# First modulation rows: eight resident units, five summed by VectorE, three multiplied by TensorE, rows read from the accumulators

## The reference, cut to what matters

```python
mod = jax.nn.silu(c) @ w_ada + b_ada            # c: 1 x 1024, w_ada: 1024 x 6144
sh1, sc1, g1, sh2, sc2, g2 = jnp.split(mod, 6)
h = rms_norm(x, norm1_g) * (1 + sc1) + sh1
proj = h @ w_in
```

## Time and profile before

| | |
|---|---|
| Median of three runs | 2128.17 us (2126.04 to 2130.38) |
| The profiled execution | 2135.76 us, span 2132.9 us |
| TensorE busy | 1873.9 us (88%), 10004 records |
| VectorE busy | 1362.5 us (64%) |
| ScalarE busy | 911.1 us (43%) |
| DMA over the span | 403.91 MB, 189 GB/s |

### The profile page before, as it was taken

One profiled execution on the slowest core, in us unless ns is written; L12 is line 12 of the kernel. 1 busy time (PEld: TensorE's weight loads), 2 busy tenths in 40 slices (PEclk: granted clock), 3 DMA queues, 4 the chain that ended last, 5 costly groups with the idle time before them and its releaser, 6 DMA issues.

```text
span 2132.9 us, 25755 instructions
## 1 busy us (share of the span) xinstructions
PE 1873.9 (88%) x10004; PEld 1610.2 (75%) x10004; DVE 1362.5 (64%) x1848; ACT 911.1 (43%) x951; POOL 87.0 (4%) x101
## 2 busy tenths in 40 slices
PE   1897895688979989999999999979987779999997
PEld 0676774467869867999999999878966568878875
DVE  5458767655889855555555555556854368887885
ACT  1354423231123334444444444445533346666664
POOL 0000100000000033111000000000000000000000
PEclk9898956698989999999999999989987879999999
DMA  6543342341325477666655555544335148898892
GB/s 233 197 177 125 131 151 108 127 158 63 141 103 177 163 244 235 205 214 203 215 179 194 179 195 180 194 162 161 118 120 196 51 162 330 321 347 330 325 349 114
DMA packets 60590, 403.91 MB, mean 189 GB/s; under 512 B 7921, under 2 KB 8337, under 8 KB 14049
## 3 DMA queue, kind: packets, MB, share of 16 engines
q1 hardware_dynamic: 50976, 370.17, 47.4%
q0 software_dynamic: 5808, 20.29, 3.3%
q10 hardware_dynamic: 3730, 12.42, 1.7%
HBM read 390.79 MB, written 12.06 MB: 189 GB/s over the span
## 4 chain that ended last, share of the span: by engine, by line
PE 79%; DVE 13%; ACT 4%; issue 3%; DMA 2%; DVEq 0%; ACTq 0%; SPq 0%
PE ps L1944 20%; PE ps L1945 20%; PE ps L1946 20%; PE ps L2022 6%; PE ps L2257 3%; DVE wlo L1032 2%; ACT whi L582 2%; DMA raw<-in_stream_dram 2%; PE ps L2106 1%; PE ps L2430 1%; PE ps L2085 1%; PE ps L2495 1%; PE ps L2316 1%; PE ps L1968 1%; DVE H L1058 1%
## 5 line engine op out<-in xcount | busy, mean ns | idle before, releaser
L1032 DVE TENSOR_TENSOR wlo<-raw,whi 128x2048 fp32r<-128x2048 f32 x186 | 425.7, 2291 | 432.8 <-ACT whi L582 432.8
L582 ACT ACTIVATE whi<-raw 128x2048 fp32r<-128x2048 f32 x186 | 356.2, 1916 | 461.5 <-PE ps L1946 418.2
L1944 PE MATMUL ps<-thi,whi 128*128 128x256 f32 x1088 | 311.1, 286 | 5.1 <-DVE tlo L1044 4.2
L1945 PE MATMUL ps<-tlo,whi 128*128 128x256 f32 x1088 | 310.3, 285 | 0.0
L1946 PE MATMUL ps<-thi,wlo 128*128 128x256 f32 x1088 | 310.1, 285 | 0.0
L1944 PE MATMUL ps<-whi,thi 128*128 128x512 f32 (+1 forms) x584 | 236.4, 405 | 32.8 <-DVE wlo L1032 25.7
L1944 PE MATMUL ps<-whi,phi 128*128 128x512 f32 x608 | 243.1, 400 | 21.4 <-DVE plo L1508 15.0
L1945 PE MATMUL ps<-wlo,phi 128*128 128x512 f32 x608 | 241.1, 396 | 0.0
L1946 PE MATMUL ps<-whi,plo 128*128 128x512 f32 x608 | 240.0, 395 | 0.0
L1945 PE MATMUL ps<-wlo,thi 128*128 128x512 f32 (+1 forms) x584 | 231.1, 396 | 0.0
L1946 PE MATMUL ps<-whi,tlo 128*128 128x512 f32 (+1 forms) x584 | 230.9, 395 | 0.0
(11 more groups left out here) (374 smaller groups left out, 2685.8 us busy)
## 6 DMA issues: line engine op xcount, KB each, us to landing
raw<-in_stream_dram SPq DMA_DIRECT2D x272, 1024.0 KB, 4.8
BIG<-in_stream_dram SPq DMA_DIRECT2D x80, 1024.0 KB, 7.1
BIG<-g_spill POOLq DMA_DIRECT2D x64, 128.0 KB, 4.6
g_spill<-H ACTq DMA_DIRECT2D x4, 1024.0 KB, 4.8
g_spill<-MOD ACTq DMA_DIRECT2D x4, 1024.0 KB, 4.9
MID<-in_gains_dram POOLq DMA_DIRECT2D x7, 512.0 KB, 4.6
s_spill<-MOD ACTq DMA_DIRECT2D x10, 256.0 KB, 4.8
MOD<-in_b_ada_dram POOLq DMA_DIRECT2D x1, 2048.0 KB, 13.6
```

The source lines that it names most:

```text
L582: nc.scalar.activation(whi[:, u % 2, :], raw[:, u % 2, :], ACT.Copy).then_inc(unit_hi, 1)
L1032: nc.vector.tensor_tensor(wlo[:, u % 2, :], raw[:, u % 2, :], whi[:, u % 2, :].bitcast(f32), ALU.subtract).then_inc(unit_split, 1)
L1944: nc.tensor.matmul(out, ahi, bhi, start=start, stop=False)
L1945: nc.tensor.matmul(out, ahi, blo, start=False, stop=False)
```

## The change

The eight units of group 0 get eight buffers: seven in BIG (empty at this time) and one in MID. SyncE issues them at once, in six transfers (units 0, 1-2, 3-4, 5, 6, 7), each with its semaphore, and behind them, with no wait, the first two units of w_in. The raw buffers and the counts of unit_split now begin with w_in (`landed`, and "- DC" in the waits). VectorE sums units 0 to 4 only. TensorE multiplies units 5, 6 and 7 directly as float32, with silu_cols as the stationary side: a 128x128 block for each unit in which every column is silu(c)'s slice (a new copy by VectorE). The sum of the five is multiplied by ones, and b_ada by a one-row matrix of ones; all go into the same four accumulators, in the order b_ada, unit 5, sum, unit 6, unit 7. The copies into MOD and the memset of the accumulator go: VectorE reads shift and scale from the accumulators, with the 1 added to the scale in the same instruction. Its order becomes: five sums, norm, modulation, tr_low of groups 0 and 1, lo(U_IN), tr_low of groups 2 and 3, lo(U_IN + 1). Several semaphores for small steps are merged into two (small_logs, small_exps), with the same waits. The diff, cut to its core:

```diff
+def landed(at):
+    return 16 * ((at - DC) // 2 + 1)
...
+        ada_raw = [big[:, c * UW:(c + 1) * UW] for c in range(DC - 1)] + [mid[:, 0:UW]]
+        ADA_LOADS = ((0, 1), (1, 3), (3, 5), (5, 6), (6, 7), (7, 8))
+        ADA_SUMMED = 5
+        silu_cols = mid[:, UW:UW + DC * P].rearrange("p (c n) -> p c n", c=DC)
+        b_ada_row = MOD[0:1, 0:UW]
+        ada_starts = {first: k for k, (first, _) in enumerate(ADA_LOADS)}
+        first_shift, first_scale = (ps[:, k:k + 2, :].rearrange("p a n -> p (a n)") for k in (0, 2))
+        ada_acc = [mid[:, 3072:3072 + UW], H[:, :, :].rearrange("p t n -> p (t n)"), big[:, 0:UW]]
...
+            for k, (first, last) in enumerate(ADA_LOADS):
+                if last - first == 1:
+                    sp.dma_start(ada_raw[first], stream[first, :, :]).then_inc(ada_loaded[k], 16)
+                else:
+                    sp.dma_start(big[:, first * UW:last * UW].rearrange("p (a n) -> p a n", n=UW),
+                                 stream[first:last, :, :].rearrange("a p n -> p a n")).then_inc(ada_loaded[k], 16)
             for k in range(2):
-                sp.dma_start(raw[:, k, :], stream[k, :, :]).then_inc(raw_loaded[k], 16)
...
+                sp.dma_start(raw[:, k, :], stream[DC + k, :, :]).then_inc(raw_loaded[k], 16)
...
-                        sp.wait_ge(unit_split, 2 * i + (k - 1 - whole))
+                        sp.wait_ge(unit_split, 2 * i + (k - 1 - whole - DC))
...
-            act.wait_ge(ada_zeroed, 1)
-            act.dma_start(ada_acc[0][0:1, :], io["b_ada"][0:UW].rearrange("(a n) -> a n", a=1)).then_inc(b_ada_loaded, 16)
+            act.dma_start(b_ada_row, io["b_ada"][0:UW].rearrange("(a n) -> a n", a=1)).then_inc(b_ada_loaded, 16)
...
-            nc.vector.memset(ada_acc[0], 0.0).then_inc(ada_zeroed, 1)
             nc.vector.memset(ones, 1.0).then_inc(ones_ready, 1)
             dve.wait_ge(siluc_ready, 1)
-            dve.wait_ge(b_ada_loaded, 16)
+            nc.vector.tensor_copy(silu_cols, siluc.unsqueeze(2).broadcast_to([P, DC, P])).then_inc(ones_ready, 1)
...
-                    if g == 0:
-                        last = nc.vector.tensor_scalar(out, got, plus, None, ALU.add)
-                    else:
-                        last = nc.vector.scalar_tensor_tensor(out, got, plus, out, ALU.add, ALU.add)
-                    last.then_inc(ada_free, 1)
-            def first_rows():
-                for u in range(3, DC):
-                    ada_sum(u)
-                ada_rows(0)
-                dve.wait_ge(ada_free, 4)
-            for u in range(3):
-                ada_sum(u)
-            norm(0, X, rows_ready, sc1, sh1, first_rows)
+                    nc.vector.scalar_tensor_tensor(out, got, plus, out, ALU.add, ALU.add).then_inc(ada_free, 1)
+            def first_sum(c):
+                if c in ada_starts:
+                    dve.wait_ge(ada_loaded[ada_starts[c]], 16)
+                if c == 0:
+                    mark(nc.vector.tensor_scalar(ada_acc[0], ada_raw[c], siluc[:, 0:1], None, ALU.mult))
+                    return
+                settle()
+                last = nc.vector.scalar_tensor_tensor(ada_acc[0], ada_raw[c], siluc[:, c:c + 1], ada_acc[0],
+                                                      ALU.mult, ALU.add)
+                if c < ADA_SUMMED - 1:
+                    mark(last)
+                else:
+                    last.then_inc(ada_summed, 1)
+            for c in range(ADA_SUMMED):
+                first_sum(c)
+            norm(0, X, None)
+            dve.wait_ge(ada_full, 1)
+            for t in range(TT):
+                settle()
+                mark(nc.vector.scalar_tensor_tensor(H[:, t, :], first_scale, 1.0, H[:, t, :], ALU.add, ALU.mult))
+                settle()
+                nc.vector.tensor_tensor(H[:, t, :], H[:, t, :], first_shift, ALU.add).then_inc(rows_ready, 1)
+            tr_low(T_H1, 0, (0, 1))
             lo(U_IN)
+            tr_low(T_H1, 0, (2, 3))
             lo(U_IN + 1)
-            tr_low(T_H1)
...
-            ada_sums(0, DC)
+            pe.wait_ge(b_ada_loaded, 16)
+            for m in range(4):
+                nc.tensor.matmul(ps[:, m, :], ones[0:1, :], b_ada_row[:, m * 512:(m + 1) * 512], start=True, stop=False)
+            pe.wait_ge(ones_ready, 2)
+            def first_unit(c):
+                if c in ada_starts:
+                    pe.wait_ge(ada_loaded[ada_starts[c]], 16)
+                for m in range(4):
+                    last = nc.tensor.matmul(ps[:, m, :], silu_cols[:, c, :], ada_raw[c][:, m * 512:(m + 1) * 512],
+                                            start=False, stop=c == DC - 1)
+                return last
+            first_unit(ADA_SUMMED)
+            pe.wait_ge(ada_summed, 1)
+            for m in range(4):
+                nc.tensor.matmul(ps[:, m, :], ones, ada_acc[0][:, m * 512:(m + 1) * 512], start=False, stop=False)
+            first_unit(ADA_SUMMED + 1)
+            first_unit(ADA_SUMMED + 2).then_inc(ada_full, 1)
```

More of the change, by code:

```diff
@@ L345, in hybrid_block_then_mixer_memory_moe_kernel @@
         siluc_ready, ones_ready = sem("siluc_ready"), sem("ones_ready")
-        ada_zeroed, b_ada_loaded, b_ada_late = sem("ada_zeroed"), sem("b_ada_loaded"), sem("b_ada_late")
+        ada_loaded, ada_summed = [sem(f"ada_loaded{k}") for k in range(len(ADA_LOADS))], sem("ada_summed")
+        b_ada_loaded, b_ada_late = sem("b_ada_loaded"), sem("b_ada_late")
         b_gate_loaded = sem("b_gate_loaded")
@@ L452, in _ @@
                 else:
-                    sp.wait_ge(unit_split, splits(u - 2) + 1)
+                    sp.wait_ge(unit_split, splits(u - 2) + 1 - DC)
                 sp.dma_start(raw[:, u % 2, :], stream[apart.get(u, u), :, :]).then_inc(raw_loaded[u % 2], 16)
@@ L461, in load @@
                 elif m >= 4:
-                    sp.wait_ge(unit_split, splits(U_MOE) + m - 5)
+                    sp.wait_ge(unit_split, splits(U_MOE) + m - 5 - DC)
                 sp.dma_start(m_raw[m % RAW_RING], unit).then_inc(m_loaded[m % RAW_RING], 16)
@@ L578, in hi @@
                 at, at_off = (u, off) if at is None else (at, at_off)
-                act.wait_ge(raw_loaded[u % 2], 16 * (at // 2 + 1) + 8 * at_off)
+                act.wait_ge(raw_loaded[u % 2], landed(at) + 8 * at_off)
                 if s >= 2:
@@ L969, in _ @@
             m_high(3)
-            act.wait_ge(r_ready, 1)
-            nc.scalar.activation(r_prob, r_log, ACT.Exp).then_inc(r_exp, 1)
+            act.wait_ge(small_logs, 3)
+            nc.scalar.activation(r_prob, r_log, ACT.Exp).then_inc(small_exps, 1)
             def gathered_high(b):
@@ L1036, in used, with tr_low @@
                 dve.wait_ge(unit_used, u - SPLIT_U + 1 + off)
-            def tr_low(t, first=0):
-                for k in range(T_GROUPS[t]):
+            def tr_low(t, first=0, groups=None):
+                for k in groups or range(T_GROUPS[t]):
                     g = T_BASE[t] + k
@@ L1046, in tr_low, with norm @@
                         ALU.subtract).then_inc(tr_lo, 1)
-            def norm(j, src, out_sem, scale=None, shift=None, meanwhile=None):
+            def norm(j, src, out_sem, scale=None, shift=None):
                 for t in range(TT):
@@ L1059, in norm @@
                                                           ALU.mult, ALU.mult)
-                    if scale is None:
+                    if out_sem is None:
+                        mark(last)
+                    elif scale is None:
                         last.then_inc(out_sem, 1)
-                        continue
-                    mark(last)
-                    if meanwhile is None:
-                        modulate(t, out_sem, scale, shift)
-                if meanwhile is not None:
-                    meanwhile()
-                    for t in range(TT):
+                    else:
+                        mark(last)
                         modulate(t, out_sem, scale, shift)
@@ L1948, in arrived @@
             def arrived(u, off=0):
-                pe.wait_ge(unit_split, splits(u) + 1 + off)
+                pe.wait_ge(unit_split, splits(u) + 1 + off - DC)
             def free_bank(n, off=0):
@@ L2016, in whole_T @@
                 if 0 in quarters:
-                    pe.wait_ge(raw_loaded[u % 2], 16 * (u // 2 + 1))
+                    pe.wait_ge(raw_loaded[u % 2], landed(u))
                 for q in quarters:
@@ L2027, in ada_sums @@
             def ada_sums(g, units):
-                pe.wait_ge(unit_split, units)
+                pe.wait_ge(unit_split, units - DC)
                 for m in range(4):
```

51 lines of the change are left out of this document (26 added, 25 removed).

## The result

The changed kernel takes 2116.28 us (median of six runs, 2110.97 to 2120.64), the kernel before 2127.11 (six runs, 2124.73 to 2131.55). The ratio is 0.9944, with a 95% interval of 0.9926 to 0.9962: 0.56% faster. In a second series of six runs beside eleven of the kernel before it was 0.9928 (0.9904 to 0.9951). I had forecast 2111.9, 16.25 us less, in a range of 2107 to 2119. The direction was right, the time is in the range, and the gain is about two thirds of the forecast by the first series.

A forecast was written before the change was run, and what follows sets the result against it. TensorE, 79% of the chain, bounds the kernel, so the stretch before its first projection product counts: 10.5 us from earlier modulation products plus 5.8 from the shorter way to projection, 16.25 off 2128.17, gives 2111.9 us; range 2107 to 2119.

The forecast's parts named there:

- T: End of TensorE's modulation products, at 48.96 us in the kernel before; forecast 38.5, with bounds 37.2 and 39.8.
- S: Start of TensorE's first projection product, at 64.90 us in the kernel before; forecast 48.65, 16.25 us sooner.
- rival (d): After S, a later transfer loses the lead again, in part or whole: 2120 to 2128 us; chance 0.04.
- I give q1 0.37 MB a us: Rate of SyncE's unit loads once only packets of 1 KB and smaller take turns with its 8 KB ones.
- the first starts cold at 15.7 and ends at 21.7: TensorE's block for b_ada's row, before T: eight records starting at the low clock, about 6.0 us long.
- the 6.8 that I had named as a sign of being wrong: TensorE's blocks before T: after the first, blocks of 3.4 us were forecast; one of 6.8 would show the forecast wrong.
- From T to S: Way from modulation products to first projection product: forecast 10.15 us for 15.94, 5.8 less, by dropped copies and VectorE's new order.
- What was said to cost nothing: Norm (3.9 us) hidden under TensorE's blocks, silu_cols copy (0.62 to 1.28) without effect, later w_in loads not late after S.
- (a): Loads before T: queues take turns by whole transfers, b_ada at 19.5, T 39.2, S 49.4, 2112.7 us; chance 0.08.
- (b): Blocks before T: all four after b_ada's run at 6.82 us, T 50.8, S 61.0, 2124.3 us; chance 0.05.
- (c): Loads before T: each queued transfer waits for the last, unit 7 at 38.8, T 42.2, S 52.4, 2115.7 us; chance 0.04.
- (e): Loads before T: the rate falls with that many queued, at 150 GB/s giving 2135.6 us, slower; chance 0.03.

The follow-up runs named there:

- late rows: ScalarE's queue issues the five small row loads only after splitting the first two w_in units, against the changed kernel; 2114.49 us (one run).
- three idle products: Three unread products behind the last modulation block, added to the kernel with small row loads late and b_ada's block over 128 rows; 2116.18 us, ratio 0.9918.

## Why the prediction was right, and where its sum was off

**The bound and the place.** Right. T and S fell, and what followed was shifted. The lead over the kernel before was 13.7 at 63 us of it, 15.4 at 211 and 16.8 at 1518 (the same ScalarE instruction in the two traces). No later transfer took it back, which was rival (d): ScalarE's first wait for raw after S is 6.9 us now and 7.5 before, and the lead grows from there.

**T, forecast 38.5 with bounds of 37.2 and 39.8, is 42.2.** This is the term that was mis-sized. X and b_ada came at 15.5 and 15.8 and the first pair of units at 15.3, where I had 15.2, 15.7 and 14.8. Two steps behind them failed. The first is "I give q1 0.37 MB a us": it was 0.31, so units 3 and 4 came at 22.07 instead of 20.7, and unit 5 at 25.67 instead of 23.5. I had taken the rate from a stretch in which the other queue's packets were 32 bytes each, and the rows to come were 1 KB. Each costs q1 a turn that is no longer free. The late rows confirm it. The second is "the first starts cold at 15.7 and ends at 21.7" with a clock that might hold over the pause. Its rise was read from a block over 128 rows, and the new block has one. It stayed low for 6.8 us of records and left unit 5's block to raise the clock; I had put half of that cost in (T was taken midway between 37.2 and 39.8). That block, 6.19 long, is close to the 6.8 that I had named as a sign of being wrong, and the pause before it was 2.70, not 1.8. Together 2.2 (unit 5 later), 1.3 (the other half of a cold block) and 0.2 make the 3.7. The upper end of the range, 2119, had been set for such a rise.

**From T to S, forecast 10.15, is 9.5.** Right, to 0.6. The four operations are 1.22 us, not 1.25, the two of different halves overlap by 0.1, and tr_low is 0.60 a group when two follow each other. The copies (2.5) and the order (3.9) were undone one at a time and add up.

**What was said to cost nothing.** The norm is hidden: it ends at 30.6, 11.6 before the accumulators are ready. The copy into silu_cols takes 0.69, in the bounds. The later issue of the third and fourth unit of w_in costs nothing: ScalarE's first wait after S is still for TensorE (8.5 us).

**From S to the time.** S is 13.2 sooner in one profile and 14.35 in the other, and the medians differ by 10.8 and 15.0. By my own rule, the median less the shift of S, a T and S as measured would have given 2115.0, against 2116.28 and 2117.0. So the time missed by as much as T did, and no other miss of that size hid it. The span of the profiled executions differs by 23.6. Of the surplus, 6.4 arises between 1641 and 1676 us of the kernel before. These are the windows, before and after:

```profile
1629.00:1674.00 45.00, 31.56 (x125) 23.95 (x124) 13.89 (x36) 14.85 (x31) 0.00 (x0) 0.72 0.42 164
```

```profile
1613.00:1658.00 45.00, 30.39 (x140) 23.66 (x139) 15.27 (x38) 16.04 (x33) 0.00 (x0) 0.89 0.42 163
```

The code there is the same, and TensorE had 0.72 and 0.89 of its clock (the stage that takes 36.7 and 30.3 us). The forecast had gone by the runs' median for the time and noted that the profiled execution lay 7.6 above it. This stretch may be most of the reason; it isn't shown, since the other runs have no profile. Another 3.6 of the surplus had come by 1518 us. How far a shift of S reaches the end can't be read from single profiles better than that: from S to the end of the span the thirteen take 2057.6 us (the changed kernel's first) to 2068.0 (the kernel before), and with the excess of this stage taken off still 2057.6 to 2064.2. The differences begin in the first 300 us behind S, and it isn't shown what they hang on. The four kernels with late rows lie at 2062.5 and above, so part of what they gain up to S may be given back there. The medians of six runs show such a loss in one of the three that were timed so (that of the three idle products).

**The rivals.** (a), whole transfers in turn, is out: b_ada landed at 15.8, not at 19.5, and the packets of 16 to 22 us are 239 to 237, mostly one and one. So with ten units queued the rows still speak against the rule of the Trainium skill's page DMA: Bandwidth & Descriptors, section Queues, rings and completion order. (b), the low clock throughout, was there for b_ada's block and for six records of unit 5's. From unit 5's on TensorE had no pause, and the clock rose. (c), one transfer after the other, had a T of 42.2, which is the T measured; that is chance. By (c) unit 7 lands at 38.8, and ScalarE split the first unit of w_in, queued behind it, at 33.28. (e) is out by the 0.31 MB a us of this kernel, and both by the 427 GB/s of the late rows.

## What to carry to other kernels

Queue loads ahead as far as buffers allow, and then look at what shares the queues: small packets in another queue take a turn each, and moving five small loads behind the big ones brought S 2 to 3 us forward here. When work is moved to a faster engine, compare it with the slower engine that has no pause: VectorE alone reached T no later than VectorE and TensorE together, as long as TensorE's first full block began at the low clock; with the clock up, the two together were 1.0 us sooner. When the way from a result to its first use is cut, order the engine in between so that each half's next step is released before long work of another kind (3.9 us here by the order of four calls).

## What the runs showed of the hardware

- A block of eight records over one row, 6.8 us of them, left TensorE at 1.2 GHz in eight profiles of eight. Behind a stretch at 2.4 GHz the granted clock fell to 1.2 GHz while such a block ran (0.77 from 16.1 to 20 us, one profile). The same block over 128 rows went to 2.4 GHz in three of three, 4 to 5 us from its start.
- After a block over 128 rows the granted clock stayed up for the whole of a pause of 4.5 us, and fell in the busy block that followed, after two records (one profile).
- Two DMA queues with work took turns of one packet whatever its size (382 of 457 from 16 to 22 us): 0.21 MB of small packets went with a fall of the other queue from 2.56 MB to 1.83.
- The granted clock reads 1.00 in the rows ahead of its first change, though the records run at the pace of 1.2 GHz (7.16 us for the block at 15.81). The spacing of the records is the safer view there.
- The same stage of unchanged code ran at 0.72, 0.77 and 0.89 of the clock in different executions and took 36.7, 33.6 and 30.3 us (two, two and nine of thirteen profiles). How much of the scatter of 9 us and more between runs of one kernel that is, no run here shows, since each kernel has one profile or two.
